# Fewer stops for small products in TensorE's hand-written order of a head loop

## The chip, the cores and the metric

The kernel runs on one core of a Trainium2 chip. The metric is the device time of one execution in microseconds; times are medians of several runs. The engines are TensorE (PE in the profile, PEld for its weight loads), VectorE (DVE), ScalarE (ACT), GpSimd (POOL) and SyncE (SP), each with a queue of its own that it works through in order; they meet only through semaphores.

## The reference

One block of a hybrid model on 512 tokens of width 2048, in float32:

```python
u = rmsnorm(h, norm_g[l])
proj = u @ w_in[l]                       # q, k, v, gates, s5 input, attention query, ...
o_a = gated_deltanet(qkv_a, beta_raw, a_raw, conv_w[l], ...)   # 8 heads of 128
o_b = s5_layer(x_b, ...)                 # complex diagonal state space, 64 groups of 16
o_c = memory_cross_attention(q_c, rmsnorm(mem, mem_norm_g[l]), w_kv_mem[l])
merged = gates[:,:,0]*p_a + gates[:,:,1]*p_b + gates[:,:,2]*p_c
h = h + merged @ w_out[l]
return rmsnorm(h, final_g)
```

For the delta rule the kernel works with four chunks of 128 tokens in a head. It needs the inverse of a triangular matrix for each chunk (made level by level: two small products, "x" and "p", on each of six levels), products of keys with keys and keys with queries, and then new values, outputs and states chunk after chunk. For the state space part it needs input products, a scan over time with cosine and sine tables, and output products.

## The kernel before

The kernel has phases: attention over the memory, then the head loop with which this case deals, then the gated unit, the three branch products and the output product.

In the head loop one pass handles ten weight blocks of `w_in` for head a. Each block is a product of 2048 x 128 weights with the 512 tokens. It is done in split precision: ScalarE copies the raw weights to a rounded high part `wh` (line 421), VectorE subtracts to get the low part `wl` (line 429), each in two halves of a block, and TensorE forms three products for each of the 16 tiles (lines 435 to 437). A block is cut into eight eighths of two tiles, so six products of 512 columns each; a pass has 80 eighths. At the first and the fifth eighth of a block (`q` 0 and 4) TensorE waits for `w_lo`, the low part of that half of the block. Eighth 52 is the fifth of block 6 (counted from zero) and eighth 56 the first of block 7; the blocks lie in two slots in turn.

In the same pass the small products of two earlier heads are woven in: those of head j, whose projections are complete (keys, values, inversion levels, s5 inputs), and those of head l, one further back (weights, new values, chunk outputs, norm, s5 outputs). `mixer(a, j, l)` on TensorE sets their order by hand: `until(e)` issues weight eighths up to e, and then the named small products follow. A stop is a place at which small products stand. The first pass of the three works on heads without small products, the next one has j alone, then come six passes in a hardware loop, one last full pass after it (head a is replaced by gate blocks), and a short one of two blocks with l alone.

All other engines have an order of their own in each pass, written by hand too. VectorE's, in the part around eighths 48 to 60, where `split(b, half)` is line 429 for block b + 1:

```python
if j: level_p(j, 2); level_t(j, 2); s5_states(j, 2, 0); level_x(j, 3)
split(5, 1)
if j: s5_states(j, 2, 1); level_p(j, 3); level_t(j, 3)
split(6, 0)
if j: level_x(j, 4)
split(6, 1)
```

`level_x` on VectorE masks the product x of a level (line 1898), `level_p` subtracts the product p (line 1903), `level_t` transposes (1910), and `s5_states` has three products in part 0, and three products and two scans in part 1 (lines 1954 to 1961). `keys`, `system` (line 1874) and `values` follow the split of block 3's second half; `first_lower` (1885, 1887), and the split of block 4's first half follow these. VectorE's last s5 part of a pass stands behind its mask of level 6, whose product TensorE issues at stop 69. GpSimd then turns the scanned states back (`turn_back`, lines 640 to 643, six instructions for each of four state groups, counted by the semaphore `dem`). Each of the four groups must be through (`dem` at 24) before TensorE may form the s5 outputs of that head (line 1026).

ScalarE takes the squares of the chunk outputs (line 1440) as soon as the fourth is there (semaphore `op` at 4). Behind this in its queue stand the copy of block 0, the splits of block 2, the decays (1406 to 1417), the s5 matrices (1386), the output root (1444), the tables and the splits of block 3.

Lines of small products in the rows: 964 weights, 975 and 977 new values, 985 to 991 chunk outputs, 908 keys with keys, 923 turn of the lower matrix, 935 level x, 948 level p, 1026 s5 outputs.

Of the kernel before, what the change touches and what calls it, by code (L numbers as in the profile page):

```python
# [85 lines left out]
def count(j, first, per):  # L86

    return j[0] * per + (first + per * j[1])


def wait(e, s, value):

    if isinstance(value, int) and value <= 0:
        return
    e.wait_ge(s, value)
# [666 lines left out]
def tensor_program(k, pe):  # L762
# [122 lines left out]
    def big(j, b, *eighths):  # L885
        for q in eighths:
            eighth(k, pe, B_MIX + b, PER, j, q, k.uh, k.ul, S, k.mx_out, B_MIX)

    def values(j):
        pe.wait_ge(k.silu, count(j, 3, 3))  # L890
        wait(pe, k.og, count(j, 0, 2))
        for n in range(NT):
            mm = pe.transpose(ps[2][:, n * P:(n + 1) * P], k.vc[:, n * P:(n + 1) * P], ident)
        mm.then_inc(k.vtr, 1)

    def keys(j):
        pe.wait_ge(k.silu, count(j, 2, 3))
        wait(pe, k.oroot, count(j, 0, 1))
        for n in range(NT):
            mm = pe.transpose(ps[6][:, n * P:(n + 1) * P], k.kc[:, n * P:(n + 1) * P], ident)  # L900
        mm.then_inc(k.ktr, 1)

    def keys_keys(j):
        pe.wait_ge(k.silu, count(j, 2, 3))
        wait(pe, k.st_s, count(j, 0, 3))
        for n in range(NT):
            c = bass.ts(n, P)
            mm = pe.matmul(ps[7][:, c], k.kc[:, c], k.kc[:, c], start=True, stop=True)
        mm.then_inc(k.kk, 1)

    def keys_queries(j):
        pe.wait_ge(k.silu, count(j, 1, 3))
        pe.wait_ge(k.vb_s, count(j, 1, 1))
        for n in range(NT):
            c = bass.ts(n, P)
            mm = pe.matmul(ps[2][:, c], k.kc[:, c], k.qc[:, c], start=True, stop=True)  # L916
        mm.then_inc(k.kq, 1)

    def turn_lower(j):
        pe.wait_ge(k.lm, count(j, 1, 1))  # L920
        pe.wait_ge(k.kb, count(j, 2, 2))
        for n in range(NT):
            mm = pe.transpose(ps[6][:, n * P:(n + 1) * P], k.dl[:, n, :], ident)
        mm.then_inc(k.ltr, 1)

    def level_x(j, l):

        pe.wait_ge(k.lt_s, count(j, 1, 1))
        if l == 1:
            pe.wait_ge(k.tu_s, count(j, 2, 3))  # L930
            pe.wait_ge(k.qkt, count(j, 1, 1))
        else:
            pe.wait_ge(k.tus, count(j, 2 * l - 3, 11))
        for n in range(NT):
            mm = pe.matmul(ps[2][:, n * P:(n + 1) * P], k.lt[:, n, :], k.tl[:, n, :], start=True, stop=True)  # L935
        mm.then_inc(k.lx, 1)
# [16 lines left out]
    def level_t(j, l):  # L953

        pe.wait_ge(k.tus, count(j, 2 * l - 1, 11))
        for n in range(NT):
            mm = pe.transpose(ps[7][:, n * P:(n + 1) * P], k.tl[:, n, :], ident)
        mm.then_inc(k.ltt, 1)

    def weights(j):  # L960

        pe.wait_ge(k.tus, count(j, 11, 11))
        for n in range(NT):
            mm = pe.matmul(ps[2][:, n * P:(n + 1) * P], k.kbg[:, n, :], k.tu[:, n, :], start=True, stop=True)  # L964
        mm.then_inc(k.wt, 1)

    def new_values(j, n):

        if n == 0:
            pe.wait_ge(k.wtn, count(j, 1, 1))  # L970
        else:
            pe.wait_ge(k.st_s, count(j, n, 3))
            pe.wait_ge(k.vn_s, count(j, n, 4))
        c = bass.ts(n, P)
        mm = pe.matmul(ps[6][:, c], k.tu[:, n, :], k.vb[:, n, :], start=True, stop=n == 0)  # L975
        if n:
            mm = pe.matmul(ps[6][:, c], k.dl[:, n, :], k.st[:, :], start=False, stop=True)
        mm.then_inc(k.vp, 1)

    def chunk_output(j, n):  # L980

        pe.wait_ge(k.vn_s, count(j, n + 1, 4))
        c = bass.ts(n, P)
        if n < NT - 1:
            pe.matmul(ps[7][:, 0:P], k.kd[:, n, :], k.vn[:, n, :], start=True, stop=True).then_inc(k.sp_s, 1)
        if n == 0:
            pe.wait_ge(k.pm, count(j, 4, 4))
            pe.wait_ge(k.qkt, count(j, 1, 1))
        mm = pe.matmul(ps[2][:, c], k.vn[:, n, :], k.du[:, n, :], start=True, stop=n == 0)
        if n:  # L990
            mm = pe.matmul(ps[2][:, c], k.st[:, :], k.qd[:, n, :], start=False, stop=True)
        mm.then_inc(k.op, 1)

    def output_norm(j):
        pe.wait_ge(k.osum, count(j, 1, 1))
        pe.matmul(ps[6][:, :], ones, k.lt[:, :, :], start=True, stop=True).then_inc(k.sso, 1)

    def s5_matrices(j):

        pe.wait_ge(k.s5_w, count(j, 13, 13))  # L1000
        pe.wait_ge(k.bp_l, count(j, 2, 2))
        wait(pe, k.mod, count(j, 0, 32))
        wait(pe, k.ysum, count(j, 0, 1))
        for n in range(2):
            for q in range(4):
                pe.transpose(ps[3 + n][:, q * P:(q + 1) * P], k.bpad[:, n, q].rearrange("p r g i -> p (r g i)"), ident)
        for n in range(2):
            mm = pe.transpose(ps[5][:, n * P:(n + 1) * P], k.cpad[:, n].rearrange("p g s -> p (g s)"), ident)
        mm.then_inc(k.s5_tr, 1)

    def s5_inputs(j, q):

        pe.wait_ge(k.bc_s, count(j, 2, 3))
        pe.wait_ge(k.x4_in, count(j, 256, 256))
        wait(pe, k.mod, count(j, 8 * q - 2, 32))
        pe.matmul(ps[3][:, :], k.bs[:, 0, q, :], k.x4[:, q, :], start=True, stop=True)  # L1016
        pe.matmul(ps[4][:, :], k.bs[:, 1, q, :], k.x4[:, q, :], start=True, stop=True).then_inc(k.bu, 1)

    def s5_outputs(j):

        pe.wait_ge(k.bc_s, count(j, 3, 3))
        pe.wait_ge(k.dem, count(j, 24, 24))
        for n, h in enumerate((k.hr, k.gr)):
            for q in range(4):
                r = slice(32 * q, 32 * q + 32)
                mm = pe.matmul(ps[5][r, :], k.bc[:, n, r], h[q][:, :], start=n == 0, stop=n == 1)  # L1026
        mm.then_inc(k.yp, 1)

    def mixer(a, j, l, blocks=PER):

        done = [0]

        def until(e):
            while done[0] < min(e, 8 * blocks):
                big(a, done[0] // 8, done[0] % 8)
                done[0] += 1

        if l: weights(l)
        until(1)
        if l: s5_outputs(l)  # L1040
        until(2)
        if l: new_values(l, 0)
        until(3)
        if l: chunk_output(l, 0)
        until(4)
        if l: new_values(l, 1)
        until(5)
        if l: chunk_output(l, 1)
        until(6)
        if l: new_values(l, 2)  # L1050
        until(7)
        if l: chunk_output(l, 2)
        until(8)
        if l: new_values(l, 3)
        until(9)
        if l: chunk_output(l, 3)
        until(10)
        if j: keys_keys(j)
        until(12)
        if j: s5_matrices(j)  # L1060
        until(13)
        if l: output_norm(l)
        until(16)
        if j: s5_inputs(j, 0)
        until(20)
        if j: keys(j)
        until(25)
        if j: values(j)
        until(28)
        if j: turn_lower(j)  # L1070
        until(29)
        if j: keys_queries(j)
        until(31)
        if j: s5_inputs(j, 1)
        until(36)
        if j: level_x(j, 1)
        until(39)
        if j: level_p(j, 1)
        until(43)
        if j: level_x(j, 2)  # L1080
        until(44)
        if j: s5_inputs(j, 2)
        until(46)
        if j: level_p(j, 2)
        until(49)
        if j: level_x(j, 3)
        until(53)
        if j: level_p(j, 3)
        until(56)
        if j: level_x(j, 4)  # L1090
        until(58)
        if j: s5_inputs(j, 3)
        until(60)
        if j: level_p(j, 4)
        until(63)
        if j: level_x(j, 5)
        until(66)
        if j: level_p(j, 5)
        until(69)
        if j: level_t(j, 5); level_x(j, 6)  # L1100
        until(74)
        if j: level_p(j, 6)
        until(80)

    pe.wait_ge(k.xa_out, 8 * XH - 1)
    for b in range(PER):
# [4 lines left out]
        big((0, 0), b, *range(3, 8))  # L1111
    pe.wait_ge(k.xa_og, 2 * XH)
    mixer((1, 0), (0, 0), None)
    with pe.Fori(2, HEADS) as i:
        mixer((i, 0), (i, -1), (i, -2))
# [1040 lines left out]
```

## Time and profile before

| what | value |
|---|---|
| median of 3 runs | 2136.77 us (2135.12 to 2136.9) |
| profiled execution | 2135.68 us, span 2134.0 us |
| TensorE busy | 2102.7 us, 99% of the span |
| VectorE busy | 1234.9 us, 58% |
| ScalarE busy | 806.2 us, 38% |
| GpSimd busy | 735.7 us, 34% |
| granted TensorE clock | 0.998 of full speed |

Busy times of matmuls overlap in the records, and their ends are modelled, so the distance from one start to the next is what a product costs. A small fp32 product of 128 columns shows as two records (x2 in a row), and four such products as x8. What stands in brackets at the end of a row is the idle time of the engine just before it, and who ended it. In such rows a start time is in microseconds from the start of the span, and the second number is the duration.

### The profile page before, as it was taken

How to read it: one execution, taken by the hardware profiler on the slowest of the kernel's cores; microseconds unless marked ns; L12 is line 12 of the kernel's file. 1: busy time of each engine (PE TensorE's matmuls, PEld its weight loads, DVE VectorE, ACT ScalarE, POOL GpSimd, SP SyncE). 2: the span in 40 equal slices, each digit the busy share in tenths (PEclk: the TensorE clock that was granted, in tenths of full speed). 3: DMA queues.
4: the chain of work that ended last, by engine and by line, in shares of the span. 5: the costliest groups of instructions: out<-in, count | busy, mean ns of one | idle time of the engine just before them, and what ended most of it. 6: DMA issues, size and time to landing. Idle time of an engine off the chain costs nothing.

```text
span 2134.0 us, 29400 instructions
## 1 busy us (share of the span) xinstructions
PE 2102.7 (99%) x10378; PEld 1751.1 (82%) x10378; DVE 1234.9 (58%) x1635; ACT 806.2 (38%) x1057; POOL 735.7 (34%) x551
## 2 busy tenths in 40 slices
PE   6999999999999999999999999999999999999998
PEld 5889888888888888888888888878878888888887
DVE  6543242338688587786877869757443344554333
ACT  5533232353343444434434345353252222222223
POOL 0000000029476484674856748559201100100000
PEclk9999999999999999999999999999999999999999
DMA  7244343443333433334334333343356555553334
GB/s 241 80 119 130 108 128 89 114 132 93 102 102 95 117 89 104 109 88 114 100 96 118 89 108 98 98 125 104 99 163 195 179 165 163 161 162 118 119 118 148
DMA packets 382570, 260.27 MB, mean 122 GB/s; under 512 B 23737, under 2 KB 351778, under 8 KB 381602
## 3 DMA queue, kind: packets, MB, share of 16 engines
q1 hardware_dynamic: 364754, 207.92, 35.1%
q0 software_dynamic: 10832, 38.80, 5.3%
q10 hardware_dynamic: 6912, 12.59, 1.6%
q8 instruction: 46, 0.75, 0.1%
q14 instruction: 26, 0.21, 0.0%
HBM read 223.59 MB, written 27.28 MB: 118 GB/s over the span
## 4 chain that ended last, share of the span: by engine, by line
PE 94%; DVE 3%; ACT 1%; issue 1%; DMA 0%; SPq 0%; POOLq 0%; ACTq 0%; DVEq 0%
PE bank L435 28%; PE bank L437 28%; PE bank L436 28%; PE bank L935 2%; PE bank L948 2%; PE bank L1026 1%; PE bank L822 1%; PE bank L837 1%; PE bank L975 0%; DVE gk L1606 0%; DVE xs L1601 0%; PE bank L1016 0%; PE bank L916 0%; PE bank L964 0%; PE bank L950 0%
## 5 line engine op out<-in xcount | busy, mean ns | idle before, releaser
L435 PE MATMUL bank<-uh,wh 128*128 128x512 f32 x2048 | 824.7, 403 | 1.1 <-ACT gk L1353 0.8
L437 PE MATMUL bank<-uh,wl 128*128 128x512 f32 x2048 | 800.2, 391 | 0.0
L436 PE MATMUL bank<-ul,wh 128*128 128x512 f32 x2048 | 798.4, 390 | 0.0
L429 DVE TENSOR_TENSOR wl<-raw,wh 128x1024 fp32r<-128x1024 f32 x352 | 469.6, 1337 | 512.9 <-ACT wh L421 511.0
L421 ACT ACTIVATE wh<-raw 128x1024 fp32r<-128x1024 f32 x352 | 369.9, 1058 | 552.6 <-DMA raw<-in_w_in_dram 174.2
L435 PEld LDWEIGHTS bank<-uh,wh 128*128 128x128 f32 x2048 | 385.3, 188 | 84.4 <-issue 10.4
L437 PEld LDWEIGHTS bank<-uh,wl 128*128 128x128 f32 x2048 | 384.4, 188 | 82.5
L436 PEld LDWEIGHTS bank<-ul,wh 128*128 128x128 f32 x2048 | 385.5, 188 | 75.3 <-issue 2.9
L599 POOL DMA_DIRECT2D gated_c<-ox x8 | 4.5, 565 | 398.3 <-DVE ox L1673 397.7
L640 POOL TENSOR_TENSOR hr<-tcos,gr 128x512 f32<-128x512 f32 x32 | 51.8, 1617 | 223.2 <-DVE gi L1961 223.0
L435 PE MATMUL bank<-gh,wh 128*128 128x512 f32 x256 | 100.8, 394 | 0.0
L437 PE MATMUL bank<-gh,wl 128*128 128x512 f32 x256 | 100.1, 391 | 0.0
L436 PE MATMUL bank<-gl,wh 128*128 128x512 f32 x256 | 99.7, 390 | 0.0
L435 PE MATMUL bank<-wh,uh 128*128 128x512 f32 x256 | 99.6, 389 | 0.0
L437 PE MATMUL bank<-wh,ul 128*128 128x512 f32 x256 | 99.6, 389 | 0.0
L436 PE MATMUL bank<-wl,uh 128*128 128x512 f32 x256 | 99.6, 389 | 0.0
L1353 ACT ACTIVATE gk<-bank 128x512 f32<-128x512 f32 x48 | 28.7, 598 | 173.4 <-PE bank L437 173.3
L717 POOL DMA_DIRECT2D gates<-gates x24 | 17.1, 713 | 208.1 <-DVE merged L2083 136.2
L435 PE MATMUL bank<-mh,wh 128*128 128x256 f32 x256 | 74.7, 292 | 2.0 <-DVE wl L429 2.0
L436 PE MATMUL bank<-ml,wh 128*128 128x256 f32 x256 | 72.7, 284 | 0.0
L437 PE MATMUL bank<-mh,wl 128*128 128x256 f32 x256 | 72.6, 284 | 0.0
L1353 ACT ACT_TABLE_LOAD x39 | 50.0, 1283 | 45.6 <-PE bank L437 45.0
(319 smaller groups left out, 2896.6 us busy)
## 6 DMA issues: line engine op xcount, KB each, us to landing
raw<-in_w_in_dram SPq DMA_DIRECT2D x224, 512.0 KB, 3.7
raw<-in_w_kv_mem_dram SPq DMA_DIRECT2D x32, 512.0 KB, 3.9
raw<-in_w_out_dram SPq DMA_DIRECT2D x32, 512.0 KB, 3.8
gates<-gk ACTq DMA_DIRECT2D x48, 256.0 KB, 4.2
gates<-gates POOLq DMA_DIRECT2D x24, 512.0 KB, 4.6
raw<-in_s_w_glu_dram SPq DMA_DIRECT2D x16, 512.0 KB, 3.9
raw<-in_w_br_c_dram SPq DMA_DIRECT2D x16, 512.0 KB, 3.9
raw<-in_w_br_a_dram SPq DMA_DIRECT2D x16, 512.0 KB, 3.9
```

The source lines that it names most:

```text
L421: act.activation(k.wh[slot][:, c], k.raw[slot][:, c], ACT.Copy).then_inc(k.w_hi, 1)
L429: dve.tensor_tensor(k.wl[slot][:, c], k.raw[slot][:, c], k.wh[slot][:, c].bitcast(F32), ALU.subtract).then_inc(k.w_lo, 1)
L435: pe.matmul(o, ah, bh, start=start, stop=False)
L436: pe.matmul(o, ah, bl, start=False, stop=False)
L437: return pe.matmul(o, al, bh, start=False, stop=stop)
L640: pool.tensor_tensor(o[:, :], c1[:, :], a[:, :], ALU.mult).then_inc(k.dem, 1)
L822: mm = pe.matmul(ps[4 + m % 2][:, 0:MEM], k.qx[:, t, m * P:(m + 1) * P], k.kt[:, t, :], start=t == 0, stop=t == 1)
L837: mm = pe.matmul(ps[2 + t][:, :], k.vx[:, m, t * P:(t + 1) * P], k.ptx[:, m, :], start=m == 0, stop=m == MT - 1)
L935: mm = pe.matmul(ps[2][:, n * P:(n + 1) * P], k.lt[:, n, :], k.tl[:, n, :], start=True, stop=True)
L948: mm = pe.matmul(ps[6][:, c], k.tu[:, n, :], k.gx[:, n, :], start=True, stop=True)
L1026: mm = pe.matmul(ps[5][r, :], k.bc[:, n, r], h[q][:, :], start=n == 0, stop=n == 1)
L1353: act.activation(k.gk[n][:, :], o[:, :], ACT.Sigmoid).then_inc(k.mx_out, 1)
```

## The change

The stops of TensorE's order in a pass are moved together. The products themselves, their number and their order among each other stay as they are, except that some of them now stand further ahead or back among the weight eighths. No other engine's program changes. Counting the one ahead of the first eighth, a full pass has 33 stops before the change and 25 after it.

```diff
-        if l: weights(l)
-        until(1)
-        if l: s5_outputs(l)
+        if l: weights(l); s5_outputs(l)
         until(2)
         if l: new_values(l, 0)
         until(3)
@@
         if l: chunk_output(l, 2)
         until(8)
         if l: new_values(l, 3)
-        until(9)
+        until(10)
         if l: chunk_output(l, 3)
-        until(10)
         if j: keys_keys(j)
-        until(12)
+        until(13)
         if j: s5_matrices(j)
-        until(13)
         if l: output_norm(l)
         until(16)
         if j: s5_inputs(j, 0)
-        until(20)
-        if j: keys(j)
-        until(25)
-        if j: values(j)
-        until(28)
-        if j: turn_lower(j)
-        until(29)
-        if j: keys_queries(j)
-        until(31)
-        if j: s5_inputs(j, 1)
+        until(24)
+        if j: keys(j); values(j)
+        until(30)
+        if j: turn_lower(j); keys_queries(j); s5_inputs(j, 1)
         until(36)
         if j: level_x(j, 1)
         until(39)
         if j: level_p(j, 1)
-        until(43)
-        if j: level_x(j, 2)
         until(44)
-        if j: s5_inputs(j, 2)
-        until(46)
+        if j: level_x(j, 2); s5_inputs(j, 2)
+        until(47)
         if j: level_p(j, 2)
-        until(49)
+        until(50)
         if j: level_x(j, 3)
         until(53)
         if j: level_p(j, 3)
-        until(56)
-        if j: level_x(j, 4)
-        until(58)
-        if j: s5_inputs(j, 3)
+        until(57)
+        if j: level_x(j, 4); s5_inputs(j, 3)
         until(60)
         if j: level_p(j, 4)
```

## Rows read from the trace of the kernel before

**Rows 1.** The page, parts 1 and 4: busy times, and the chain that ended last.

```profile
PE 2102.7 (99%) x10378; PEld 1751.1 (82%) x10378; DVE 1234.9 (58%) x1635; ACT 806.2 (38%) x1057; POOL 735.7 (34%) x551
...
PE 94%; DVE 3%; ACT 1%; issue 1%; DMA 0%; SPq 0%; POOLq 0%; ACTq 0%; DVEq 0%
```

**Rows 2.** Busy time of each engine in one pass of the head loop.

```profile
736.17:871.17 135.00, 134.84 (x688) 112.08 (x687) 102.48 (x133) 57.55 (x76) 86.00 (x59) 1.00 0.37 102
```

**Rows 3.** Timeline of TensorE at the start of a pass (start, duration, instruction).

```profile
715.36 1.05 PE L964 MATMUL bank<-tu,kbg 128*128 128x128 f32 x8
716.17 0.48 PE L435 MATMUL bank<-uh,wh 128*128 128x512 f32 x1
...
717.72 1.07 PE L1026 MATMUL bank<-hr,bc 128*32 128x512 f32 x8
...
720.85 0.39 PE L437 MATMUL bank<-uh,wl 128*128 128x512 f32 x1
721.08 0.38 PE L975 MATMUL bank<-vb,tu 128*128 128x128 f32 x2
...
721.54 0.39 PE L436 MATMUL bank<-ul,wh 128*128 128x512 f32 x1
...
722.47 0.39 PE L437 MATMUL bank<-uh,wl 128*128 128x512 f32 x1
```

**Rows 4.** Timeline: GpSimd's last state product, twice, and TensorE in the short pass.

```profile
715.47 1.28 POOL L643 TENSOR_TENSOR gr<-gr,karg 128x512 f32<-128x512 f32 x1 [0.18 <-POOL karg L641]
...
1526.43 1.28 POOL L643 TENSOR_TENSOR gr<-gr,karg 128x512 f32<-128x512 f32 x1
...
1526.74 1.05 PE L964 MATMUL bank<-tu,kbg 128*128 128x128 f32 x8
```

**Rows 5.** Timeline of TensorE around eighths 49 to 56 of the same pass.

```profile
799.70 0.40 PE L437 MATMUL bank<-uh,wl 128*128 128x512 f32 x1
799.93 1.05 PE L935 MATMUL bank<-tl,lt 128*128 128x128 f32 x8
...
801.05 0.40 PE L436 MATMUL bank<-ul,wh 128*128 128x512 f32 x1
...
806.28 1.05 PE L948 MATMUL bank<-gx,tu 128*128 128x128 f32 x8
...
811.28 1.05 PE L935 MATMUL bank<-tl,lt 128*128 128x128 f32 x8
```

**Rows 6.** Timeline of VectorE in the same stretch.

```profile
801.02 0.69 DVE L1898 TENSOR_TENSOR gx<-bank,cst 128x512 f32<-128x512 f32 x1 [1.58 <-PE bank L935]
801.63 1.59 DVE L429 TENSOR_TENSOR wl<-raw,wh 128x1024 fp32r<-128x1024 f32 x1
...
809.05 1.31 DVE L429 TENSOR_TENSOR wl<-raw,wh 128x1024 fp32r<-128x1024 f32 x1
```

**Rows 7.** Timeline of the first pass that has small products: TensorE, then VectorE.

```profile
529.92 1.05 PE L935 MATMUL bank<-tl,lt 128*128 128x128 f32 x8
...
531.69 1.21 DVE L429 TENSOR_TENSOR wl<-raw,wh 128x1024 fp32r<-128x1024 f32 x1
...
538.75 1.22 DVE L429 TENSOR_TENSOR wl<-raw,wh 128x1024 fp32r<-128x1024 f32 x1
```

**Rows 8.** Timeline of ScalarE after the last chunk output.

```profile
735.21 0.60 ACT L1440 ACTIVATE lt<-bank 128x512 f32<-128x512 f32 x1 [1.25 <-PE bank L991]
```

**Rows 9.** Timeline of the last full pass: TensorE, then VectorE.

```profile
1441.60 0.66 PE L923 MATMUL bank<-cst,dl 128*128 128x128 f32 x4 [1.40 <-DVE dl L1874]
...
1448.99 0.40 PE L435 MATMUL bank<-uh,wh 128*128 128x512 f32 x1
...
1440.87 0.68 DVE L1874 TENSOR_TENSOR dl<-bank,dl 128x512 f32<-128x512 f32 x1
...
1445.67 2.31 DVE L429 TENSOR_TENSOR wl<-raw,wh 128x1024 fp32r<-128x1024 f32 x1
```

**Rows 10.** TensorE's wait ahead of the fourth new values in a pass.

```profile
732.62 0.49 PE L975 MATMUL bank<-vb,tu 128*128 128x128 f32 x2 [0.16 <-DVE st L1921]
```

## Prediction

> **What bounds the kernel now.** I read the page first. TensorE is busy 99% of the span, and the chain that ended last runs through it for 94% [rows 1]. So only two things can move the time: how long TensorE's own instructions take, and how long it waits. I then cut one pass of the head loop out of the trace, from one product of the keys to the next. It lasts 135.00 us, with TensorE busy for 134.84 us at full granted clock (2.4 GHz) [rows 2]. A pass holds 480 weight products. In a dense stretch they start every 0.227 us: from 801.05 to 806.28 there are 23, so 0.2274 each, 1.36 us for an eighth of six [rows 5]. 480 of them are 109 us, and the small products take nearly all of the other 26 us. TensorE stands still once per pass, before the fourth "new values", where it waits for a state from VectorE; the profile calls that 0.16 us [rows 10].
>
> The reader should see that the small products are packed with no visible gap. A stop at a new place can then cost only what is hidden in the distance between starts, and every stop that is moved can turn into a wait.
>
> **What a place costs by itself.** A place with one fp32 product (two records of 128 columns): from the last weight product before it (720.85) to the second after it (721.54) is 0.69 us; less two spacings of 0.227 this is 0.24 us [rows 3]. A place with four products (eight records): 799.70 to 801.05 is 1.35 us, less 0.454 is 0.90 us [rows 5]. The difference is 0.66 us for six records, so 0.11 us a record, and 0.24 less two records leaves 0.02 us for the place. The four weight products after 721.54 take 0.93 us in place of 0.91 [rows 3], 0.02 more. So a place costs 0.04 us on top of its products. It is no more than that, because a small product's weights are loaded behind the product before it.
>
> The change takes away 8 of 33 stops in a full pass (I count 33 and 25 with the one at zero). One of the eight (the s5 outputs) is reckoned below. Seven times 0.04 is 0.28 us in each of the six passes of the middle loop, 1.7 us; five stops in the first pass give 0.2 us, the last full pass 0.1 us. Gain: 2.0 us. All moved products stay the same in number and size, and none issues a DMA; SyncE's and GpSimd's queues hold the same instructions.
>
> **First moved wait: the s5 outputs at zero.** They wait for GpSimd's last product of the fourth state group, which starts at 715.47 and takes 1.28 us: ready at 716.75 [rows 4]. Now they stand one eighth behind the weights product (715.36) and start at 717.72, a microsecond after that [rows 3]. In the change they stand directly behind it, where TensorE is free at 716.17. So TensorE waits there. It is the next thing in its queue, with the whole of the pass behind it. The lag from an end to a start in such a wait is 0.05 us (1440.87 + 0.68 to 1441.60) [rows 9]; I add 0.05 us for weights that are no longer loaded ahead. Start in the change: 716.85. That is 0.87 us earlier than now, but the eighth that stood ahead of it comes after it, 1.36 us. Net loss 0.49 us, its own saved place already counted. GpSimd's chain hangs on a TensorE stop much earlier (the sixty-ninth eighth), which isn't moved, so the gap comes in every pass. Seven times 0.49 is 3.4 us; in the short last pass GpSimd ends at 1527.71 and the weights product starts at 1526.74, 0.97 us in place of 1.39 us [rows 4], so 0.07 us. Sum 3.5 us. Bounds: 0 if the wait is met in time, 0.9 a pass if GpSimd ends 0.4 us later.
>
> **Second moved wait: level 3's product from 49 to 50.** VectorE works in order. Behind the mask of level 3 (which waits for this product) are queued the split for the second half of the sixth block, the second part of a state group with two scans, level 3's subtraction and transpose, and then the split for the seventh block, which TensorE needs at eighth 56. Now that row of work runs from 801.02 to 809.05 + 1.31 = 810.36 [rows 6], that is 10.43 us after the product's start at 799.93 [rows 5]. TensorE has until 811.28, where another small place comes first, and then the eighth: no wait. In the change the product comes one eighth later, and the place ahead of eighth 56 (level 4) is moved behind it. From the product's start to eighth 56 are then 811.28 - 799.93 - 1.36 = 9.99 us. VectorE needs 10.43 us and 0.1 us of lag: a wait of 0.54 us. In six passes: 3.2 us. In the first pass the same chain is shorter: product at 529.92, last split until 538.75 + 1.22 = 539.97, so 10.05 us and a wait of 0.16 us [rows 7]; I take the same for the last full pass. Sum 3.5 us. Bounds: 0.16 us a pass everywhere (1.3 us in all) and 1.3 us a pass with the slow splits below.
> Eighth 52 sits on the same row: its split ends at 803.22 [rows 6], in the change 1.36 us later, 804.58; eighth 52 starts 17 spacings after 801.05, at 804.92 [rows 5]. It passes with 0.3 us to spare, and I take nothing.
>
> What is late next: level 4's mask and all behind it on VectorE by some 2 us at most, met by the idle time that VectorE has before each later mask (1.58 us before this one [rows 6]); from the sixty-ninth eighth on all is in step with TensorE again.
>
> **Third moved wait: the last chunk output from 9 to 10.** ScalarE takes its square as soon as it is there: it had been idle for 1.25 us and TensorE released it [rows 8]. Behind it in ScalarE's queue are the query's copy, two splits, the decays and the output root, and VectorE's queue waits for these; both run 1.36 us later from here to the middle of the pass. In the middle passes the splits that TensorE needs have more room than that. In the last full pass they haven't: there TensorE already waits 1.40 us for the lower matrix, and VectorE's split that follows ends at 1445.67 + 2.31 = 1447.98, for the eighth that starts at 1448.99 [rows 9]. Moving the turn from 28 to 30 dissolves the 1.40 us, but the split then ends at 1449.34 and TensorE goes on at 1449.44 at the earliest, 0.45 us later than now. If VectorE were not late there, TensorE would go on at 1448.1, a gain of 0.9 us. I take +0.5 us, once, since this queue follows ScalarE.
>
> Moving keys to 24, values to 24, level 2 to 44 and 47 costs nothing: what waits for them on VectorE comes later than their new places.
>
> **Sum:** 3.5 + 3.5 + 0.5 - 2.0 = +5.5 us. The profiled execution took 2135.68 us around a span of 2134.0 us and would take 2141.2 us; the median of the three runs is 1.1 us above the profiled one, and on that the forecast is 2142.3 us.
>
> **A rule weighed.** The split of the sixth block's second half takes 1.59 us beside GpSimd's work in a middle pass [rows 6] but 1.21 us in the first pass [rows 7], and a split of the same size in the last full pass takes 2.31 us [rows 9]. The Trainium skill, GPSIMD Engine Reference, section Key points, says that GpSimd shares its SBUF interfaces with VectorE and contends with VectorE instructions that have two SBUF inputs. The split has two, so the trace agrees. By that rule the size of the second wait depends on how the shifted work of the two engines falls together; the two rivals below that differ in it are worked out from the rows alone.
>
> **Rivals.**
> - Both waits come (the forecast): +5.5 us, 2142.3 us. Chance 0.53.
> - The wait at eighth 56 shrinks, as VectorE's row of work takes 10.05 us as in the first pass: 8 x 0.16 = 1.3 us in place of 3.5 us. Sum +3.3 us, 2140.1 us. For it: that row exists; against it: the row of middle passes repeats, and GpSimd's work is shifted by the same 1.36 us as VectorE's. Chance 0.17.
> - The splits fall on GpSimd's work and take 2.31 us in place of 1.59 us: 0.7 us more at eighth 56 in each of six passes, +4.3 us. Sum +9.8 us, 2146.6 us. Chance 0.16.
> - The other side, not slower: the products that are waited for are ready in time. At zero this decides at 716.2 us: were GpSimd's chain ready 0.6 us earlier, the s5 outputs would follow without a wait. With the wait at eighth 56 at 1.3 us this gives 1.3 + 0.5 - 2.0 - 8 x 0.04 = -0.5 us, 2136.3 us; with the last full pass's 1.40 us dissolved too, 2134.9 us. Against it: 715.47 + 1.28 is the same in relation to TensorE in each middle pass. Chance 0.11.
> - The change saves more than 0.04 us a place, because the products after a place pick up speed as well. It would have to be 0.1 us a place more, some 6 us in all, to cancel the waits and leave the time as it is; the rows leave no room for it. Chance 0.03.
>
> **How the numbers follow.** The range runs from 2137.5 us, between the not-slower case and the small wait, to 2147.0 us, which takes in the slow splits. 0.2% is 4.3 us, about what a measurement of this kernel tells from no change. Slower by more needs 2141.05 us: most of the forecast's chance and all of the slow splits', 0.47 + 0.16 and little of the small wait's, 0.65. Same: 0.31. Faster: 0.04.
>
> **What would show it.** Right: TensorE's first s5 output starts some 1.5 us after the weights product, with a wait put down to GpSimd; a wait for the split before eighth 56 in seven passes, 0.5 us in six of them; the pass of the loop at 135.8 us in place of 135.0 us; the 1.40 us wait for the lower matrix gone and a wait for a split in its place. Wrong: a pass of 134.7 us would say that neither wait came; a pass above 136.3 us would say that splits are slow or that a wait comes at a place I hold for free (eighth 52, or the stop at 39).

## The result, and the profile after

The changed kernel took 2147.8 us (median of 6 runs, 2146.62 to 2148.93), the kernel before, on the same chip, 2136.64 us (2135.12 to 2137.25): ratio 1.0054, 95% interval 1.0043 to 1.0064. It is slower, as forecast, but by 11.2 us and not by 5.5 us, and the time lies just above the range. The profiled span is 2145.7 us, 11.7 us more than before.

First the page of the changed kernel, parts 1 and 4:

```profile
PE 2104.1 (98%) x10378; PEld 1751.9 (82%) x10378; DVE 1237.6 (58%) x1635; ACT 805.3 (38%) x1057; POOL 742.7 (35%) x551
...
PE 84%; DVE 8%; POOL 3%; issue 3%; ACT 1%; DMA 1%; SPq 0%; POOLq 0%; DVEq 0%; ACTq 0%
```

Against [rows 1], TensorE's share of the chain that ended last has gone from 94% to 84%, and VectorE and GpSimd have come into it with 8% and 3%. TensorE is as busy as before; the added time is waiting. One middle pass, from the weight product before stop 0 to the next such (span, then busy time of PE, PEld, DVE, ACT, POOL):

```profile
717.20:853.60 136.40, 134.83 (x687) 112.19 (x686) 102.73 (x132) 57.37 (x75) 87.10 (x60) 1.00 0.38 101
```

So 136.40 us in place of 135.00 [rows 2]. TensorE's waits by who ended them (total, times, longest):

```profile
PE bank L435 <- DVE wl L429: 9.8, 12, 1.7
...
PE bank L1026 <- POOL gr L643: 2.9, 8, 0.5
...
PE bank L435 <- ACT gk L1339: 1.7, 2, 1.0
PE bank L975 <- DVE st L1907: 1.0, 6, 0.2
```

Before, the first of these was 2.0 us in two waits, the second did not exist, and there was one of 1.4 us for the lower matrix [rows 9] that is now gone. TensorE in a middle pass, at stop 0, at level 3's product and ahead of eighth 56:

```profile
717.44 1.05 PE L964 MATMUL bank<-tu,kbg 128*128 128x128 f32 x8
718.88 1.06 PE L1026 MATMUL bank<-hr,bc 128*32 128x512 f32 x8 [0.39 <-POOL gr L643]
...
803.52 1.05 PE L935 MATMUL bank<-tl,lt 128*128 128x128 f32 x8
...
813.27 0.39 PE L437 MATMUL bank<-uh,wl 128*128 128x512 f32 x1
814.67 0.50 PE L435 MATMUL bank<-uh,wh 128*128 128x512 f32 x1 [1.01 <-DVE wl L429]
```

Both forecast waits are there. From 813.27 to 814.67 is 1.40 us, 1.17 us more than the usual spacing of 0.227 us; I call this the wait at eighth 56. The step forecast 0.54 us. VectorE's row of work in the same stretch:

```profile
804.61 0.69 DVE L1884 TENSOR_TENSOR gx<-bank,cst 128x512 f32<-128x512 f32 x1 [1.39 <-PE bank L935]
805.22 1.22 DVE L429 TENSOR_TENSOR wl<-raw,wh 128x1024 fp32r<-128x1024 f32 x1
...
808.39 2.18 DVE L1947 TENSOR_TENSOR_SCAN gr<-s5h,gr 128x512 f32<-128x512 f32 x1
810.49 1.56 DVE L1947 TENSOR_TENSOR_SCAN gi<-s5h,gi 128x512 f32<-128x512 f32 x1
...
813.30 1.31 DVE L429 TENSOR_TENSOR wl<-raw,wh 128x1024 fp32r<-128x1024 f32 x1
```

From mask to the end of the last split: 813.30 + 1.31 - 804.61 = 10.00 us, against 9.34 us in [rows 6] (810.36 - 801.02). GpSimd at the same time, in its instructions for the arguments of the fourth group's tables:

```profile
799.86 0.69 POOL L619 TENSOR_SCALAR karg<-cst,s5h 128x512 f32<-128x512 f32 x1 [0.36 <-POOL gr L643]
...
805.24 2.63 POOL L626 TENSOR_SCALAR karg<-cst,s5h 128x512 f32<-128x512 f32 x1 [0.21 <-POOL farg L624]
808.05 1.44 POOL L628 TENSOR_TENSOR farg<-farg,karg 128x512 f32<-128x512 f32 x1 [0.18 <-POOL karg L626]
```

In the kernel before, these were (same view; the scans beside them in VectorE's rows below it):

```profile
801.45 1.57 POOL L626 TENSOR_SCALAR karg<-cst,s5h 128x512 f32<-128x512 f32 x1 [0.20 <-POOL farg L624]
...
805.17 1.51 DVE L1961 TENSOR_TENSOR_SCAN gr<-s5h,gr 128x512 f32<-128x512 f32 x1
806.61 1.19 DVE L1961 TENSOR_TENSOR_SCAN gi<-s5h,gi 128x512 f32<-128x512 f32 x1
```

The reader should see two things. The two scans take 3.74 us in place of 2.70. And L626, of the same size in both, starts 0.18 us ahead of the split in the kernel before (801.45 and 801.63) and takes 1.57 us; after, it starts 0.02 us behind it and takes 2.63 us. What follows is about these 0.2 us.

### The profile page after: what moved, and what is told of

It reads as the page before. It is cut to its first block, busy times and chain, and to the rows that moved or that the text cites. A ratio compares the mean times of both kernels' runs of the same rounds, so it can differ in the third digit from the quotient of the medians.

```text
span 2145.7 us, 29400 instructions
## 1 busy us (share of the span) xinstructions
PE 2104.1 (98%) x10378; PEld 1751.9 (82%) x10378; DVE 1237.6 (58%) x1635; ACT 805.3 (38%) x1057; POOL 742.7 (35%) x551
## 4 chain that ended last, share of the span: by engine, by line
PE 84%; DVE 8%; POOL 3%; issue 3%; ACT 1%; DMA 1%; SPq 0%; POOLq 0%; DVEq 0%; ACTq 0%
PE bank L435 25%; PE bank L437 24%; PE bank L436 24%; PE bank L935 2%; DVE wl L429 2%; POOL karg L641 1%; PE bank L948 1%; DVE gi L1947 1%; POOL hr L643 1%; PE bank L1026 1%; PE bank L822 1%; PE bank L837 1%; DVE gr L1947 1%; DVE gi L1943 1%; DMA yst<-s_out 1%
## 5 line engine op out<-in xcount | busy, mean ns | idle before, releaser
L429 DVE TENSOR_TENSOR wl<-raw,wh 128x1024 fp32r<-128x1024 f32 x352 | 464.6, 1323 | 520.2 <-ACT wh L421 518.4
```

The costliest lines, as they stand in the source:

```text
L429: dve.tensor_tensor(k.wl[slot][:, c], k.raw[slot][:, c], k.wh[slot][:, c].bitcast(F32), ALU.subtract).then_inc(k.w_lo, 1)
```

## The experiments

The runs ask for each of the two waits by itself, then which move makes the second, then whether GpSimd is behind it and by what rule. Ratios are to the kernel before, in runs on the same chip; the chip is not the same in all experiments, so two of them are best compared by their ratios and passes. A "middle pass" is one of the six in the hardware loop.

**1. The s5 outputs alone.** The kernel before with the first edit only:

```diff
-        if l: weights(l)
-        until(1)
-        if l: s5_outputs(l)
+        if l: weights(l); s5_outputs(l)
```

> The kernel before with one part of the change: the s5 outputs stand directly behind the weights product, ahead of the first eighth. Theory A (each moved wait has its own price and they add): a wait for GpSimd of 0.4 us at this stop in eight passes, the pass of the loop at 135.45 us in place of 135.00 us, +3.5 us in all, and no wait at eighth 56. Theory B (the waits of the changed kernel come together, because GpSimd's and VectorE's work is thrown out of step by the first one): splits or scans of 2 us and waits appear elsewhere too, and the time rises by 6 us or more.

2139.47 us, ratio 1.0015 (1.0004 to 1.0026), span 2138.7. Middle passes 135.43 to 135.47 us, so +0.45 us each where the step said 0.49, and no wait at eighth 56. This wait is what the prediction said, and is not what was missing.

**2. The changed kernel with this edit undone.**

> The changed kernel with the s5 outputs back at stop 1. Theory A: the wait for GpSimd goes, the wait of 1.17 us at eighth 56 stays as it is, the pass of the loop is 135.94 us, 3.5 us less than the changed kernel in all. Theory B: the wait at eighth 56 shrinks too, to the 0.54 us of the forecast, and the kernel is 7 us faster than the changed one.

2144.71 us, ratio 1.0040 (1.0024 to 1.0056). Pass 135.97 us, and the wait at eighth 56 unchanged at 1.17 us. The two waits add up; neither feeds the other.

**3. The changed kernel with the fourth chunk output back at 9**, and **4. with level 3's product back at 49.**

```diff
-        until(10)
+        until(9)
         if l: chunk_output(l, 3)
+        until(10)
         if j: keys_keys(j)
```
```diff
-        until(50)
+        until(49)
         if j: level_x(j, 3)
```

> The changed kernel with the last chunk output back at stop 9 (keys with keys stay at 10). ScalarE, and after it GpSimd and VectorE, are some 1.36 us earlier to the middle of the pass, but level 3's product and the stops around eighth 56 are untouched. Theory A (the size of the wait at eighth 56 is set by how GpSimd's table arguments fall on VectorE's scans): the two scans leave 2.18 and 1.56 us, VectorE's row of work from the mask to the split changes from 10.0 us by several tenths, and the wait at eighth 56 changes with it, to anything between 0.2 and 1.2 us. Theory C (the wait is set by the distance of the stops alone): row of work and wait stay at 10.0 us and 1.17 us in the middle passes. Both expect the wait for a split in the last full pass (1.2 us) to go, as VectorE is no longer late there.

> The changed kernel with level 3's product back at stop 49. VectorE's row of work starts 1.36 us earlier against eighth 56. Theory A and C: at least 1.17 us of wait in each of the six middle passes is gone or down to the 0.1 us that a longer overlap may leave, the pass of the loop is 135.2 to 135.3 us, 7 us less than the changed kernel in all. If the wait at eighth 56 did not hang on this product but on the last split alone, the time would stay.

Run 3: 2139.99 us, ratio 1.0019 (1.0008 to 1.0031); middle pass 135.43 us, wait at eighth 56 down from 1.17 to 0.14 us, last full pass 136.95 us in place of 138.33. Run 4: 2143.75 us, ratio 1.0038 (1.0022 to 1.0053); pass 136.14 us, wait still 0.90 us. This turned my step round: by it the 49 to 50 was the cause and the chunk output cost nothing in a middle pass. VectorE and GpSimd in run 3:

```profile
804.46 1.22 DVE L429 TENSOR_TENSOR wl<-raw,wh 128x1024 fp32r<-128x1024 f32 x1
...
807.63 1.52 DVE L1948 TENSOR_TENSOR_SCAN gr<-s5h,gr 128x512 f32<-128x512 f32 x1
809.07 1.19 DVE L1948 TENSOR_TENSOR_SCAN gi<-s5h,gi 128x512 f32<-128x512 f32 x1
...
803.62 1.57 POOL L626 TENSOR_SCALAR karg<-cst,s5h 128x512 f32<-128x512 f32 x1 [0.21 <-POOL farg L624]
```

L626 is 0.84 us ahead of the split, both are quick, and so are the scans. In run 4 VectorE's row started early but met GpSimd's work head on (split 2.17 us, scans 2.18 and 1.56): it needed 10.96 us and ate most of what the earlier start had given.

**5. Both back at once.**

> The changed kernel with both the fourth chunk output back at 9 and level 3's product back at 49. Each alone took 0.97 and 0.26 us off the changed pass of 136.40 us. Theory A (VectorE's row of work is late by what the product is late, plus what GpSimd's arguments for the fourth table cost on the scans): with both back the row is as before, no wait for a split ahead of eighth 56, and the pass is the changed one less 1.15 us: 135.0 of before, plus 0.45 for the s5 outputs, less 0.2 for merged stops, 135.2 to 135.3 us; the last full pass near 136.9 us; span 2137.3 us, time 2138.3 us. Rival B (the two moves act independently and a wait of some other source stays at eighth 56): 136.40 - 0.97 - 0.26 = 135.17 us or a wait left over of 0.1 us; Rival C (level 3's move is what matters once the chunk output is back and vice versa): the same as A. What tells more is whether the scans take 1.5 and 1.2 us and the wait is nil.

2136.96 us, ratio 1.0004 (0.9993 to 1.0015); middle passes 135.24 to 135.33 us, no wait at eighth 56. The scans took 2.19 and 1.56 us, not the 1.5 and 1.2 that I expected: the row (10.17 us) is no shorter than in the changed kernel, but it now starts early enough. So the two moves are not independent, and the chunk output is not the only move that makes the row long. Counted from the start of the pass, L626 is 0.89 us later here than in the kernel before and the split 0.21 us. GpSimd's queue starts its work for these tables when ScalarE's table for an earlier group is there, and ScalarE now waits for the s5 matrices, which the change moved from 12 to 13 and no step of the prediction priced. ScalarE in run 5:

```profile
744.08 1.08 ACT L1373 ACTIVATE bs<-bank 128x512 fp32r<-128x512 f32 x2 [0.36 <-PE bank L1008]
```

**6. The chunk output's move alone**, in the kernel before:

```diff
-        until(9)
-        if l: chunk_output(l, 3)
         until(10)
+        if l: chunk_output(l, 3)
         if j: keys_keys(j)
```

> The kernel before with one edit: the fourth chunk output moved from 9 to 10, so that it stands with the keys' products. Theory A (ScalarE takes the squares of this output, and its queue hands the delay of 1.36 us on to GpSimd's arguments for the fourth table, which then fall on VectorE's scans): scans of some 2.2 and 1.5 us in place of 1.5 and 1.2 us, VectorE's row of work longer by 0.7 us or more, and a wait for the split ahead of eighth 56 of 0.4 to 0.9 us in the middle passes: pass 135.4 to 135.8 us, span 2137 to 2139.5 us. Rival B, my prediction's step (the move costs nothing in the middle passes): pass 134.96 us, only the last full pass longer by 0.5 us, span 2134.3 us. If GpSimd's arguments, which are later by 1.36 us while the mask is not, fall past the scans, A would see them slow the splits instead.

2137.63 us, ratio 1.0009 (0.9998 to 1.0021), span 2134.5. Theory A was right on the scans (2.19 and 1.56 us, split 2.11) and wrong on the wait: passes 134.86 to 134.87 us. The row takes 10.92 us and ends at 811.47; eighth 56 starts at 811.62, so it passes with 0.1 us. In the last full pass the delay shows openly, twice the 1.40 us of [rows 9]:

```profile
1441.98 0.66 PE L923 MATMUL bank<-cst,dl 128*128 128x128 f32 x4 [2.80 <-DVE dl L1873]
```

**7. GpSimd's work shifted.** The changed kernel with one small write on GpSimd (0.10 us; the arguments behind it start 0.26 us later in the pass) ahead of the fourth group's arguments, and with three (three columns in place of one):

```diff
+            if q == 3:
+                for _ in range(1):
+                    pool.memset(k.stat[:, 36:37], 1.0)
             ts(k.karg[:, :], k.tvec, hi_, ROUND, ALU.mult, ALU.add).then_inc(k.args, 1)
```

> The changed kernel with one very small GpSimd instruction (it sets an unused column of 128 values) ahead of the fourth table's arguments, nothing else. It delays GpSimd's seven argument instructions by 0.1 to 0.2 us against VectorE. Theory A (the size of the wait at eighth 56 is set by how these instructions fall on VectorE's split and scans): the durations of split and scans change out of all proportion to the delay, back to those of the kernel before (scans of 1.5 and 1.2 us, split 1.6 us), and the wait in the six middle passes falls from 1.17 us towards 0.54 us. Theory C (the distance of the stops alone): the wait stays at 1.17 us within 0.05 us and the time within 1 us.

> As the run before with three such small instructions, so a delay of 0.3 to 0.6 us. Theory A: yet another pair of durations, a wait somewhere between 0.2 and 1.3 us, not proportional to the delay. Theory C: 1.17 us as before.

One write: 2149.54 us, ratio 1.0065 (1.0046 to 1.0083), wait at eighth 56 1.6 us (split 1.65, scans 2.18 and 1.56). Three: 2147.98 us, ratio 1.0058 (1.0039 to 1.0076), wait 1.17 us in four middle passes and 1.6 in two, so not in proportion to the delay. Theory A had said that the wait falls towards 0.54 us with one write; it rose. GpSimd's work matters, but these two (two executions each) don't yet say by what rule.

**8. GpSimd's work taken away.** The changed kernel with the seven argument instructions of the fourth group on 16 columns in place of 512 (the seven instructions then take `ka`, `fa` and `tv`; it leaves out most of that group's table):

```diff
+            ka, fa, tv = k.karg[:, :], k.farg[:, :], k.tvec
+            if q == 3:
+                ka, fa, tv = ka[:, 0:16], fa[:, 0:16], tv[:, 0:16]
```

> The changed kernel with GpSimd's seven instructions for the arguments of the fourth group's tables working on 16 columns in place of 512 (it leaves out 496 of 512 times of the angles of that group, which then hold the third group's values). TensorE's order and every other instruction stay. Theory A (contention with these instructions lengthens VectorE's split and scans): split for the sixth block 1.2 us, scans about 1.2 us each, VectorE's row from the mask of level 3 to the split of the seventh block 8.7 us in place of 10.7 us and more, no wait ahead of eighth 56, pass 136.40 - 1.17 = 135.23 us, span 2137.5 us or a little less. Rival B (the wait comes from the queue's order and the product's move, whatever GpSimd does): the wait stays at 0.5 us or more, pass 135.7 us or more, span over 2140.5 us.

2137.97 us, ratio 1.0008 (0.9996 to 1.0019). VectorE's row, at TensorE's order of the changed kernel:

```profile
802.37 0.69 DVE L1887 TENSOR_TENSOR gx<-bank,cst 128x512 f32<-128x512 f32 x1 [1.66 <-PE bank L938]
802.98 1.22 DVE L429 TENSOR_TENSOR wl<-raw,wh 128x1024 fp32r<-128x1024 f32 x1
...
806.16 1.23 DVE L1950 TENSOR_TENSOR_SCAN gr<-s5h,gr 128x512 f32<-128x512 f32 x1
807.30 1.20 DVE L1950 TENSOR_TENSOR_SCAN gi<-s5h,gi 128x512 f32<-128x512 f32 x1
...
809.75 1.31 DVE L429 TENSOR_TENSOR wl<-raw,wh 128x1024 fp32r<-128x1024 f32 x1
```

8.69 us, no wait at eighth 56, middle passes 135.0 to 135.15 us. The scans' own time is 1.2 us each; all above it is GpSimd's. Rival B is out.

**9. More work on the late row.** If it matters which of split and L626 starts first, then delaying the split should shorten the row. First with two one-column writes on VectorE between mask and split, then with one of 160 columns, for which a spare tile `k.scr` is allotted; its edit is:

```diff
         if j: level_p(j, 2); level_t(j, 2); s5_states(j, 2, 0); level_x(j, 3)
+        if j: dve.memset(k.scr[:, :], 0.0)
         split(5, 1)
```

> The changed kernel with work added to the very row that is late: two one-column writes on VectorE between the mask of level 3 and the split for the sixth block, which push the split and all behind it back by some 0.1 to 0.25 us. In the changed kernel the split starts at 805.22 and GpSimd's instruction beside it at 805.24, and takes 2.63 us; in the kernel before GpSimd's starts 0.18 us ahead of the split and takes 1.57 us. Theory A (of the two instructions the one that starts second is held back; GpSimd, held back by the split, then falls on the first scan): with the split later, GpSimd's instruction is first and takes 1.57 us, the split 1.4 to 1.6 us, the scans 1.52 and 1.19 us, and VectorE's row from the mask to the last split shrinks from 10.00 us to 9.4 to 9.6 us although it has more to do: the wait at eighth 56 falls by 0.4 to 0.6 us, pass 135.8 to 136.0 us, span 2142.5 us. Rival B (the lengths come from the mean overlap, the order of the starts means nothing): scans stay at 2.18 and 1.56 us, the row grows by what is added, the wait to 1.3 to 1.4 us, pass 136.55 to 136.65 us, span 2147 us.

> The changed kernel with one write of 160 columns to a spare place on VectorE between the mask of level 3 and the split for the sixth block (the two one-column writes of the run before ran beside the split and did not delay it). It is meant to push the split and all behind it back by some 0.15 to 0.3 us. Theory A (of the two instructions the one that starts second is held back): GpSimd's instruction now starts first and takes 1.57 us instead of 2.63, the split 1.4 to 1.6 us, the scans 1.52 and 1.19 us, and VectorE's row from the mask to the last split is 9.4 to 9.6 us instead of 10.00 us although it has more to do: the wait at eighth 56 falls by 0.4 to 0.6 us, pass 135.8 to 136.0 us, span 2142.5 us. Rival B (mean overlap, the order of the starts means nothing): scans stay at 2.18 and 1.56 us, the row grows by what is added, pass 136.55 to 136.75 us, span 2147 us or more.

The small writes ran beside the split and did not delay it (0.62 us behind the mask, as before); the pass stayed at 136.4 to 136.5 us, the time at 2147.32 us, ratio 1.0052 (1.0029 to 1.0074). That run tells nothing. The larger one:

```profile
802.13 0.69 DVE L1885 TENSOR_TENSOR gx<-bank,cst 128x512 f32<-128x512 f32 x1 [1.50 <-PE bank L936]
802.80 0.19 DVE L1991 MEMSET scr<- 128x160 f32 x1
802.91 1.50 DVE L430 TENSOR_TENSOR wl<-raw,wh 128x1024 fp32r<-128x1024 f32 x1
...
806.37 1.51 DVE L1948 TENSOR_TENSOR_SCAN gr<-s5h,gr 128x512 f32<-128x512 f32 x1
807.80 1.19 DVE L1948 TENSOR_TENSOR_SCAN gi<-s5h,gi 128x512 f32<-128x512 f32 x1
...
810.25 1.31 DVE L430 TENSOR_TENSOR wl<-raw,wh 128x1024 fp32r<-128x1024 f32 x1
...
802.65 1.57 POOL L627 TENSOR_SCALAR karg<-cst,s5h 128x512 f32<-128x512 f32 x1 [0.21 <-POOL farg L625]
```

GpSimd's instruction is now 0.26 us ahead of the split and takes 1.57 us, the scans are back at 1.51 and 1.19, and the row takes 9.43 us with one instruction more in it, 0.57 us less than without. The wait at eighth 56 is 0.52 us, the pass 135.77 us, the time 2145.47 us, ratio 1.0045 (1.0029 to 1.0060). Work added to the late engine made each middle pass 0.63 us shorter and the kernel 2.3 us faster, by these medians. The intervals of the two ratios overlap, so the passes carry this and not the time. Rival B had the scans at 2.18 and 1.56 us and a longer pass.

**10. What a stop costs, and a better order.** The kernel before with six stops more (keys and values one product at a time at 17 to 20 and 22 to 25), and with eight stops fewer, joined at the earlier place wherever the inputs were there, and with chunk output 9 and level 3's 49 left alone:

```diff
-        if l: weights(l)
         until(1)
-        if l: s5_outputs(l)
+        if l: weights(l); s5_outputs(l)
@@
         until(9)
         if l: chunk_output(l, 3)
-        until(10)
         if j: keys_keys(j)
         until(12)
         if j: s5_matrices(j)
-        until(13)
         if l: output_norm(l)
@@
         until(20)
-        if j: keys(j)
-        until(25)
-        if j: values(j)
-        until(28)
-        if j: turn_lower(j)
+        if j: keys(j); values(j)
         until(29)
-        if j: keys_queries(j)
-        until(31)
-        if j: s5_inputs(j, 1)
+        if j: turn_lower(j); keys_queries(j); s5_inputs(j, 1)
@@
         until(43)
-        if j: level_x(j, 2)
-        until(44)
-        if j: s5_inputs(j, 2)
+        if j: level_x(j, 2); s5_inputs(j, 2)
@@
         until(56)
-        if j: level_x(j, 4)
-        until(58)
-        if j: s5_inputs(j, 3)
+        if j: level_x(j, 4); s5_inputs(j, 3)
```

> The price of a stop by itself: the kernel before with the four turns of the keys at 17, 18, 19, 20 and those of the values at 22, 23, 24, 25, one at each, in place of four at 20 and four at 25. Six stops more in each full pass, same products, last ones where they were. Theory A (0.04 us a stop): pass of the loop 135.24 us, +1.7 us in all. Theory D (the 0.02 us after a stop would come anyway): 135.1 us, +0.7 us.

> A version of my own, from the kernel before: as many stops fewer (33 to 25), but each joined pair stands where no engine's queue gets later: weights and s5 outputs together at 1, last chunk output and keys with keys at 9, s5 matrices and output norm at 12, keys and values at 20, lower matrix, keys with queries and s5 inputs at 29, level 2 and s5 inputs at 43, level 4 and s5 inputs at 56. Theory A (a stop costs 0.04 us, the rest of the change's loss is waits): pass of the loop 134.7 us, no new wait, 2 us faster than the kernel before, up to 1 us more from the shorter wait in the last full pass, 2133.5 us in all. Theory D (stops cost nothing, or less than 0.02 us): pass at 134.9 to 135.0 us and no difference in time.

Six more: 2138.2 us, ratio 1.0010 (0.9999 to 1.0020), pass 135.17 us: 0.17 / 6 = 0.03 us a stop. Eight fewer: 2132.73 us (11 runs) against 2135.8 us, ratio 0.9983 (0.9974 to 0.9992), pass 134.63 to 134.65 us: 0.36 / 8 = 0.045 us a stop. This order is faster than both kernels. Its scans are slow too (2.20 and 1.56 us), with the chunk output at 9 and level 3's product at 49: here the stops saved ahead of the split are by themselves enough to lose the lead. But the row has the room.

## Why the forecast had the direction and not the size

One middle pass of each kernel at this place, read from timelines like those above; the other five have the same scans within 0.02 us. "Lead" is by how much L626 starts ahead of the split (minus: behind it); "row" is from mask to the end of the last split:

```
kernel                     lead   L626  split  scans        row    wait at 56
before                     0.18   1.57  1.59   1.51, 1.19    9.34  0
run 10, six stops more     0.39   1.57  1.38   1.52, 1.19    9.14  0
run 1, s5 outputs alone    0.24   1.57  1.53   1.51, 1.19    9.29  0
run 3, chunk output back   0.84   1.57  1.22   1.52, 1.19    8.97  0.14
run 9, 160-column write    0.26   1.57  1.50   1.51, 1.19    9.43  0.52
run 2, s5 outputs back     0.01   2.65  1.21   2.18, 1.56   10.01  1.17
changed kernel            -0.02   2.63  1.22   2.18, 1.56   10.00  1.17
run 9, one-column writes  -0.02   2.64  1.22   2.18, 1.56   10.03  1.20
run 10, eight stops fewer -0.07   2.58  1.21   2.20, 1.56   10.02  0
run 7, three, four passes -0.23   2.42  1.22   2.18, 1.56   10.01  1.17
run 5, both back          -0.50   2.32  1.37   2.19, 1.56   10.17  0
run 7, one write          -0.77   2.31  1.65   2.18, 1.56   10.42  1.60
run 6, chunk output alone -1.24   2.31  2.11   2.19, 1.56   10.92  0
run 4, level 3 back       -1.29   2.31  2.17   2.18, 1.56   10.96  0.90
run 8, 16 columns          none   0.33  1.22   1.23, 1.20    8.69  0
```

Where GpSimd's instruction leads, it is through with L628 before the scans; where the split leads, GpSimd is held back for 0.7 to 1.1 us and its next instruction falls on the first scan. Starts that are 0.02 us apart or less go the slow way whichever the record puts first; the smallest lead with quick scans is the 0.18 us of the kernel before, so that kernel stood 0.2 us from the edge. The trace shows who crossed it. In the pass the split's mask moved with TensorE and kept the saving of all merged stops ahead of it (by 1.51 us from the pass's start), GpSimd's L619, whose chain ScalarE's tables start, kept little of it (1.71 us): 0.2 us, and the lead is gone.

The wait follows by the prediction's own sum. In the changed kernel TensorE gives VectorE 9.98 us from level 3's product (803.52) to where eighth 56 was due (813.27 + 0.227), as forecast (9.99). VectorE takes 1.09 us to the mask and 10.00 us for the row, 11.09 us where the step put 10.43: with 0.05 us of lag, a wait of 1.16 us.

By the steps:

- **The bound, and that the change costs waits and saves little: right.** TensorE's busy time is the same within 1.4 us.
- **A stop is worth 0.04 us: right.** 0.03 (run 10, six more) and 0.045 us (eight fewer).
- **First moved wait, 0.49 us a pass: right,** 0.45 us in run 1, and it adds to the rest (run 2).
- **Second moved wait: right in place, half its size.** The step that failed is "VectorE needs 10.43 us": it took VectorE's row as fixed. The row took 0.66 us more, 11.09 us from the product, and the wait was 1.17 us where the step put 0.54. With it failed a reason given in the rival of the small wait, that GpSimd's work is shifted by the same 1.36 us as VectorE's. They are shifted by different amounts, 0.2 us apart, and that is enough. The 0.54 us is not the price of this move alone either: with the chunk output back, the row takes 8.97 us and the move leaves 0.14 us (run 3).
- **Third moved wait: wrong that the middle passes have room enough for it.** In the kernel before it costs them nothing (run 6), by 0.1 us. In the changed kernel it is the larger part of the wait: undone, it gives back 0.97 us a pass (run 3), and with level 3's product back at 49 it still costs 0.8 to 0.9 us (run 4 against run 5). The rows of runs 4 and 6 are equally long, 10.96 and 10.92 us; what differs is level 4's product. In run 6 it stands ahead of eighth 56, in run 4 behind it:

```profile
810.81 1.05 PE L935 MATMUL bank<-tl,lt 128*128 128x128 f32 x8
811.62 0.48 PE L435 MATMUL bank<-uh,wh 128*128 128x512 f32 x1
...
811.97 0.39 PE L437 MATMUL bank<-uh,wl 128*128 128x512 f32 x1
813.09 0.50 PE L435 MATMUL bank<-uh,wh 128*128 128x512 f32 x1 [0.73 <-DVE wl L429]
```

  From level 3's product to eighth 56 run 6 has 811.62 - 799.46 = 12.16 us and run 4 has 811.97 + 0.227 - 800.85 = 11.35 us. The prediction counted this move, but in the second wait's sum only. In the last full pass, put at +0.5 us, the 1.40 us wait went as forecast, and waits for splits came in its place, two long ones and two short:

```profile
1450.97 0.50 PE L435 MATMUL bank<-uh,wh 128*128 128x512 f32 x1 [1.09 <-DVE wl L429]
1459.32 0.47 PE L435 MATMUL bank<-uh,wh 128*128 128x512 f32 x1 [0.67 <-ACT gk L1339]
...
1498.79 0.47 PE L435 MATMUL bank<-uh,wh 128*128 128x512 f32 x1 [0.16 <-DVE wl L429]
```

  The second is put down to ScalarE; VectorE's split for it ran from 1456.86 for 2.31 us and ended at 1459.17, so it was a split as well.
- **First pass, +0.16 us at eighth 56: low,** it is 0.37 us over a spacing; and eighth 52, which I held free, waits too, 0.48 us over a spacing. Its split took 2.29 us against 1.21 in [rows 7]: GpSimd's L628 starts at 532.79 and the split at 532.89. Run 7 with three writes puts the split ahead there; it takes 1.22 us, and the two waits are nil and 0.19 us.
- **The rivals.** Nearest came the one in which VectorE's instructions fall on GpSimd's work: it put +0.7 us on eighth 56, by a split of 2.31 us. The price was right by luck (0.63 us more than the forecast's): the instruction was not the one it named. The split got quicker (1.22 us, 0.37 less) and the scans slower (1.04 more).

Sum over the span: the first pass +0.9 us (forecast 0.0), six middle passes +8.3 (4.5), the last full pass +1.95 (1.0), the rest +0.6 (0.1): 11.75 us in place of 5.6, which its rounded terms made 5.5.

Shown by runs: that both waits add, that GpSimd's arguments make the row long, that the order of the starts decides in the middle passes, and that the chunk output's move and level 3's each carry part of the wait at eighth 56, the chunk output's the larger. Only read from the trace, with no run that undoes it alone: what level 4's place behind eighth 56 and the s5 matrices at 13 add, and the share of each short wait in the last full pass.

## What to carry to other kernels

Merging stops of an in-order queue is worth about what a stop costs (0.04 us here), so join them at the earlier place, and only where no other engine's queue gets later by it: one chunk output moved by one eighth went through ScalarE's queue into GpSimd's and came back as 1 us a pass on VectorE. Before a duration is taken from the trace as fixed, look at which instructions of the engine that it contends with (here VectorE and GpSimd) stand beside it, and at how far apart their starts are; if that is less than what the change shifts, price both orders. And room of 0.1 us behind a late engine is not room: the chunk output's move fitted by that much in the kernel before, and cost 0.8 us and more where another move had taken 0.8 us of room away.

## What the hardware did that I had not expected

- Of a VectorE instruction with two inputs in SBUF and a GpSimd instruction that overlap, the one that starts second is held back; with starts 0.02 us apart or less it was GpSimd's, whichever the record puts first (runs 2 and 9). Split first by 0.02 us: GpSimd's tensor-scalar 2.63 us in place of 1.57, the split 1.22 us, its time without GpSimd beside it. GpSimd's tensor-tensor first (run 6: 800.90 to 802.19, split from 801.16): the split 2.11 us, 0.89 us more for 1.03 us of overlap. The Trainium skill, SBUF — State Buffer, section Who interferes with whom, says this: a VectorE instruction with two SBUF inputs contends with a GpSimd instruction that reads SBUF, and the one that issues first holds the shared interface while the other blocks. The traces agree on the order. They differ on the amount where GpSimd's tensor-scalar is first: in the kernel before the split lost 0.37 us for 1.39 us of overlap, and in run 3 nothing for 0.73 us. The measurement decides: this pair blocks in one direction only in part.
- A VectorE instruction with one of its two inputs in PSUM is not held back: the mask of level 3 takes 0.69 us beside GpSimd's L626 in run 3 (803.85, beside 803.62 to 805.19) and 0.69 us with nothing beside it in run 8.
- The scan, whose inputs are one tensor and one column spread over time, is held back too: 1.23 us alone, up to 2.20 us behind a tensor-tensor of GpSimd.
- Two one-column writes on VectorE (0.07 us) ran beside the split that followed them and delayed nothing; one of 160 columns (0.19 us) delayed it by 0.17 us.
